# Forget sums and mask as a bias tile added with the maxima, and the gates' product between query chunks

## What is computed

```python
kvf = rmsnorm(h, kv_norm_g) @ w_kvf            # keys, values and 16 gate columns
log_f = log_sigmoid(kvf[..., 2 * D:] + b_f)
fcum = cumsum(transpose(log_f), axis=-1)       # (heads, tokens)
q = split_heads(rmsnorm(h, fox_pre_g) @ fox_w_q)
logits = q @ k.T / 8 + fcum[t] - fcum[s]       # masked to s <= t
h = h + rmsnorm(merge_heads(softmax(logits) @ v) @ fox_w_o, fox_post_g)
```

## Time and profile before

| | us |
|---|---|
| median of 3 runs (868.89 to 869.74) | 869.2 |
| the profiled execution | 869.43 |
| its span | 867.7 |
| PE busy | 853.5 (98%) |
| DVE busy | 677.7 (78%) |
| ACT busy | 524.2 (60%) |
| POOL busy | 65.3 (8%) |

### The profile page before, as it was taken

How to read it: one execution, slowest core, us unless ns; L and a number is a source line. 1 busy time by engine, 2 the same in 40 slices (tenths; PEclk the granted TensorE clock), 3 DMA queues, 4 the chain that set the end, 5 groups by cost and what they waited for, 6 DMA issues and landing times.

```text
span 867.7 us, 15051 instructions
## 1 busy us (share of the span) xinstructions
PE 853.5 (98%) x5782; PEld 750.6 (87%) x5782; DVE 677.7 (78%) x994; ACT 524.2 (60%) x766; POOL 65.3 (8%) x128
## 2 busy tenths in 40 slices
PE   8999999999999999999999999999999999999997
PEld 8999889888888889999898888888878779998885
DVE  5767569898887987566589878889888877699684
ACT  6666657765655774667486655656746757542552
POOL 2354100000000010010010000000000001000000
PEclk9999999999999999999999999999999999999999
DMA  8445335555545345424456465455263344462321
GB/s 298 189 148 188 119 124 197 216 186 204 192 161 225 146 159 206 146 98 146 146 206 242 147 224 207 150 202 187 101 224 136 115 141 150 156 229 88 122 97 48
DMA packets 21976, 144.62 MB, mean 167 GB/s; under 512 B 2831, under 2 KB 3103, under 8 KB 5280
## 3 DMA queue, kind: packets, MB, share of 16 engines
q1 hardware_dynamic: 20448, 139.47, 44.5%
q0 software_dynamic: 1328, 4.32, 1.6%
q10 hardware_dynamic: 144, 0.04, 0.0%
HBM read 142.78 MB, written 1.05 MB: 166 GB/s over the span
## 4 chain that ended last, share of the span: by engine, by line
PE 83%; DVE 9%; ACT 3%; issue 2%; DMA 1%; POOL 0%; SPq 0%; DVEq 0%; POOLq 0%; ACTq 0%
PE psC L2033 15%; PE psC L1941 11%; PE psC L1943 10%; PE psC L1942 10%; PE psC L2036 8%; PE psD L1941 5%; PE psD L1943 5%; PE psD L1942 5%; DVE w_lo L1116 2%; PE psC L2063 2%; PE psC L2065 2%; PE psC L2072 2%; DVE arena L1330 2%; DMA raw<-stream 1%; PE psD L2355 1%
## 5 line engine op out<-in xcount | busy, mean ns | idle before, releaser
L1116 DVE TENSOR_TENSOR w_lo<-raw,w_hi 128x2048 fp32r<-128x2048 f32 x125 | 285.7, 2287 | 54.1 <-ACT w_hi L561 53.3
L561 ACT ACTIVATE w_hi<-raw 128x2048 fp32r<-128x2048 f32 x125 | 238.4, 1911 | 65.2 <-PE psC L1943 31.7
L2033 PE MATMUL psC<-xT,w_hi 128*128 128x512 f32 x640 | 200.8, 395 | 0.0
L2036 PEld LDWEIGHTS psC<-xT,w_lo 128*128 128x128 f32 x640 | 120.2, 188 | 28.3
L2036 PE MATMUL psC<-xT,w_lo 128*128 128x256 f32 x640 | 125.7, 278 | 0.0
L2033 PEld LDWEIGHTS psC<-xT,w_hi 128*128 128x128 f32 x640 | 98.6, 189 | 1.2
L1941 PE MATMUL psC<-xT,w_hi 128*128 128x256 f32 x320 | 91.6, 286 | 0.0
L1942 PE MATMUL psC<-xT,w_hi 128*128 128x256 f32 x320 | 90.5, 283 | 0.0
L1943 PE MATMUL psC<-xT,w_lo 128*128 128x256 f32 x320 | 90.5, 283 | 0.0
L1941 PE MATMUL psD<-w_hi,oT_hi 128*128 128x512 f32 x208 | 81.4, 391 | 0.6 <-DVE oT_lo L1344 0.6
L1942 PE MATMUL psD<-w_lo,oT_hi 128*128 128x512 f32 x208 | 81.0, 389 | 0.0
(11 more groups left out here) (338 smaller groups left out, 1535.6 us busy)
## 6 DMA issues: line engine op xcount, KB each, us to landing
raw<-stream SPq DMA_DIRECT2D x130, 1024.0 KB, 4.8
gbc<-post_g POOLq DMA_DIRECT2D x6, 512.0 KB, 4.7
h<-x_in SPq DMA_DIRECT2D x2, 512.0 KB, 4.5
raw<-stream SPq DMA_DIRECT2D x4, 256.0 KB, 6.3
out<-h SPq DMA_DIRECT2D x3, 256.0 KB, 2.0
arena<-b_in POOLq DMA_DIRECT2D x1, 640.0 KB, 5.8
out<-h SPq DMA_DIRECT2D x2, 128.0 KB, 2.0
pv<-pvec POOLq DMA_DIRECT2D x1, 176.0 KB, 4.4
```

The source lines that it names most:

```text
L561: nc.scalar.activation(w_hi[:, slot, :], raw[:, raw_slot, :], ACT.Copy).then_inc(hi_done, 1)
L1116: V.tensor_tensor(w_lo[:, slot, :], raw[:, raw_slot, :], w_hi[:, slot, :].bitcast(F32), ALU.subtract).then_inc(lo_done, 1)
L2033: MM(psC[:, up_bank(e, a), :], hi[:, k, a * P:a * P + P], xT[:, kk_, :, :].rearrange("p i t -> p (i t)"), start=(kk_ == 0), stop=False, sk ...
L2036: ins = MM(psC[:, up_bank(e, a), 0:T], lo[:, k, a * P:a * P + P], xT[:, kk_, 0, :], start=False, stop=(kk_ == KT - 1), skip_group_check=True)
```

## The change

The forget sums no longer go through PE. DVE writes the negated sums of 16 rows to `ftmp`; POOL stores them to memory (`f_rows`) and spreads them with four transfers over all 128 partitions into `f_bias` (384 columns for each of 16 heads, 4 heads a transfer); the first 128 columns and the last 128 of each head are written with the triangle's mask by affine_select. DVE's pair_max then has one form: it waits for the logits and for the group's bias, reads the logits from PSUM, adds the bias tile and takes the maximum in one instruction, as in the window attention. ACT's take_logits, POOL's mask_logits and PE's forget_rows are gone, and with them the selection matrix, the second copy of the gate columns and the zeroing on POOL. The gates' product is moved ahead of the second query chunk. DVE makes `wf_lo` right after the spread of the scales, and the evacuation of the second query chunk comes behind the running sum; the splits move one unit around these steps. The logits' first matmul in a bank now starts the accumulation.

```diff
-        bf_sb = sb("bf_sb", [F2, 1])
+        bf_sb = sb("bf_sb", [H, 1])
+        wf_r = sb("wf_r", [P, 2, KT * H], F32R)
...
-        wf_sb = region(4608, KT * F2).rearrange("p (k n) -> p k n", k=KT)
-        o_flat = [a[:, :, :].rearrange("p k t -> p (k t)") for a in (oT_hi, oT_lo)]
-        wf_hi, wf_lo = (o_flat[1][:, KT * F2 * i:KT * F2 * (i + 1)].rearrange("p (k n) -> p k n", k=KT) for i in range(2))
-        sel = arena[:, 5632:7680].rearrange("p (h n) -> p h n", h=H)
-        ftmp = arena[0:F2, 8576:9344].rearrange("p (i t) -> p i t", t=T)
-
-
-        neg_f_all = o_flat[1][:, 6 * T:6 * T + P + T]
-        neg_f = neg_f_all[:, P:P + T]
-        sel_r = o_flat[0].rearrange("p (h n) -> p h n", h=H)
+        wf_sb = region(4608, KT * H).rearrange("p (k n) -> p k n", k=KT)
+        wf_hi, wf_lo = (wf_r[:, i, :].rearrange("p (k n) -> p k n", k=KT) for i in range(2))
+        ftmp = arena[0:H, 9984:10752].rearrange("p (i t) -> p i t", t=T)
+
+
+        f_bias = region(3840, 384 * H).rearrange("p (h n) -> p h n", h=H)
+        f_rows = nc.dram_tensor("f_rows", (H, T), F32, kind="Internal").ap()
...
-            nc.gpsimd.memset(wf_sb, 0.0).then_inc(pool_step, 1)
-            nc.gpsimd.memset(bf_sb[:, :], 0.0).then_inc(pool_step, 1)
...
-            nc.gpsimd.memset(sel, 0.0).then_inc(pool_step, 1)
...
-            for base in (0, -32):
-
-                keep(sel, ALU.not_equal, 1.0, base, [[-1, H], [0, P]], 1).then_inc(pool_step, 1)
-                done += 1
-                pool.wait_ge(pool_step, done)
...
-            def mask_logits(p):
-
-                pool.wait_ge(sm[0]["taken"], p + 1)
-                for a in (0, 2 * P):
-                    ins = keep(pair_p[p % 3][:, :, a:a + P], ALU.is_ge, NEG, 0, [[0, 2], [-1, P]], 1)
-                ins.then_inc(sm[0]["masked"], 1)
+            def forget_bias():
+
+                pool.wait_ge(forget["cum"], 1)
+                pool.dma_start(f_rows, ftmp[:, 2, :]).then_inc(forget["stored"], 16)
+                pool.wait_ge(forget["stored"], 16)
+                for g in range(4):
+                    heads_ = slice(4 * g, 4 * g + 4)
+                    pool.dma_start(f_bias[:, heads_, P:384], f_rows[heads_, :].partition_broadcast(P)).then_inc(forget_spread[g], 16)
+                for g in range(4):
+                    heads_ = slice(4 * g, 4 * g + 4)
+                    pool.wait_ge(forget_spread[g], 16)
+                    nc.gpsimd.affine_select(out=f_bias[:, heads_, 0:P], in_=f_bias[:, heads_, P:2 * P], compare_op=ALU.is_ge, fill=NEG,
+                                            base=0, pattern=[[0, 4], [-1, P]], channel_multiplier=1)
+                    keep(f_bias[:, heads_, 2 * P:384], ALU.is_ge, NEG, 0, [[0, 4], [-1, P]], 1).then_inc(forget["masked"], 1)
 
             for i in range(1, 4):
                 pre_scales(i)
                 next_gain(i)
                 if i == 2:
-                    for p in range(H // 2):
-                        mask_logits(p)
+                    forget_bias()
...
-            def take_logits(p):
-
-                s = sm[0]
-                act.wait_ge(s["logit"], p + 1)
-                if p >= 3:
-                    act.wait_ge(s["turned"], p - 2)
-                nc.scalar.activation(pair_p[p % 3], psD[:, 2 * (p % 2):2 * (p % 2) + 2, 0:384], ACT.Copy).then_inc(s["taken"], 1)
...
-            split_to(U0["fox_kv"] + 2)
-
-            act.wait_ge(unit_done, U0["fox_q"] + 4)
-            act.wait_ge(small_loaded, 16 * 6)
+            act.wait_ge(small_loaded, 16 * 4)
             nc.scalar.activation(wf_hi, wf_sb, ACT.Copy).then_inc(consts_act, 1)
-            act.wait_ge(consts_pool, N_CONSTS)
-            nc.scalar.activation(sel_r, sel, ACT.Copy).then_inc(forget["sel"], 1)
-            split_to(U0["fox_kv"] + 3)
+            split_to(U0["fox_kv"] + 1)
             act.wait_ge(forget["bias"], 1)
             settle(nc.scalar.activation(ftmp[:, 1, :], ftmp[:, 1, :], ACT.Exp, scale=-1.0))
             nc.scalar.activation(ftmp[:, 1, :], ftmp[:, 1, :], ACT.Ln, bias=1.0).then_inc(forget["ln"], 1)
...
-                dve.wait_ge(s["logit" if w else "masked"], p + 1)
+                dve.wait_ge(s["logit"], p + 1)
                 if w == 0:
-                    z = pair_p[p % 3]
-                    V.tensor_reduce(mx[:, w, pair, 0], z[:, :, 0:P], AX.X, ALU.max)
-                    settle(V.tensor_reduce(mx[:, w, pair, 1], z[:, :, P:384], AX.X, ALU.max))
-                    V.tensor_scalar(nmx[:, w, pair, :], mx[:, w, pair, :], -1.0, None, ALU.mult).then_inc(s["max"], 1)
-                    return
+                    dve.wait_ge(forget["masked"], p // 2 + 1)
                 if p >= 3:
                     dve.wait_ge(s["turned"], p - 2)
                 for r in range(2):
+                    i = 2 * p + r
                     for q, (a, b) in enumerate(((0, P), (P, 384))):
-                        ins = V.tensor_tensor_reduce(pair_p[p % 3][:, r, a:b], psD[:, at + r, a:b], mask_window[:, a:b], 1.0, NEG,
-                                                     ALU.add, ALU.max, accum_out=mx[:, w, 2 * p + r, q:q + 1])
+                        ins = V.tensor_tensor_reduce(pair_p[p % 3][:, r, a:b], psD[:, at + r, a:b],
+                                                     mask_window[:, a:b] if w else f_bias[:, i, a:b], 1.0, NEG,
+                                                     ALU.add, ALU.max, accum_out=mx[:, w, i, q:q + 1])
                 settle(ins)
+                if w == 0:
+                    V.tensor_scalar(nmx[:, w, pair, :], mx[:, w, pair, :], -1.0, None, ALU.mult).then_inc(s["max"], 1)
+                    return
...
+            dve.wait_ge(consts_act, 3)
+            V.tensor_tensor(wf_lo, wf_sb, wf_hi.bitcast(F32), ALU.subtract).then_inc(consts_dve, 1)
             split_to(U0["fox_q"] + 4)
             evac_features("fox_q", 0, qT, QSCALE)
-            split_to(U0["fox_kv"] + 2)
-            dve.wait_ge(consts_act, 3)
-            V.tensor_tensor(wf_lo, wf_sb, wf_hi.bitcast(F32), ALU.subtract).then_inc(consts_dve, 1)
-            evac_features("fox_q", 1, qT, QSCALE)
-            settle(V.tensor_scalar(neg_f_all, region(5632, 384), 0.0, None, ALU.mult))
-
+            split_to(U0["fox_kv"] + 1)
             dve.wait_ge(forget["product"], 1)
-            settle(V.tensor_tensor(ftmp[:, 0, :], psD[0:F2, 2, 0:T], scale_row[0:F2, :], ALU.mult))
+            settle(V.tensor_tensor(ftmp[:, 0, :], psD[0:H, 2, 0:T], scale_row[0:H, :], ALU.mult))
             settle(V.tensor_scalar(ftmp[:, 0, :], ftmp[:, 0, :], bf_sb[:, :], None, ALU.add))
             magnitude(ftmp[:, 1, :], ftmp[:, 0, :]).then_inc(forget["bias"], 1)
-            split_to(U0["fox_kv"] + 3)
+            split_to(U0["fox_kv"] + 2)
             dve.wait_ge(forget["ln"], 1)
             settle(V.scalar_tensor_tensor(ftmp[:, 2, :], ftmp[:, 0, :], 0.0, ftmp[:, 1, :], ALU.min, ALU.subtract))
-            settle(V.tensor_tensor_scan(ftmp[:, 1, :], ones_row[0:F2, :], ftmp[:, 2, :], 0.0, ALU.mult, ALU.add))
-            settle(V.tensor_scalar(neg_f[0:F2], ftmp[:, 1, :], -1.0, None, ALU.mult))
-            settle(V.scalar_tensor_tensor(neg_f[32:F2], ftmp[32:F2, 1, :], -1.0, neg_f[32:F2].bitcast(F32), ALU.mult, ALU.subtract))
-            V.tensor_copy(neg_f_all[0:F2, 0:P], neg_f[0:F2, 0:P].bitcast(F32)).then_inc(forget["cum"], 1)
+            settle(V.tensor_tensor_scan(ftmp[:, 1, :], ones_row[0:H, :], ftmp[:, 2, :], 0.0, ALU.mult, ALU.add))
+            V.tensor_scalar(ftmp[:, 2, :], ftmp[:, 1, :], -1.0, None, ALU.mult).then_inc(forget["cum"], 1)
+            evac_features("fox_q", 1, qT, QSCALE)
+            split_to(U0["fox_kv"] + 3)
             fox_keys(0)
             fox()
...
+            def forget_product():
+
+                pe.wait_ge(consts_dve, 2)
+                out = psD[0:H, 2, 0:T]
+                for b in range(4):
+                    pe.wait_ge(kv_hi_done, b + 1)
+                    for k in (2 * b, 2 * b + 1):
+                        MM(out, wf_hi[:, k, :], xT_hi[:, k, :], start=(k == 0), stop=False, skip_group_check=True)
+                        MM(out, wf_lo[:, k, :], xT_hi[:, k, :], start=False, stop=False, skip_group_check=True)
+                    pe.wait_ge(kv_lo_done, b + 1)
+                    for k in (2 * b, 2 * b + 1):
+                        ins = MM(out, wf_hi[:, k, :], xT_lo[:, k, :], start=False, stop=(k == KT - 1), skip_group_check=True)
+                ins.then_inc(forget["product"], 1)
...
-                def forget_rows(g):
-
+                def logits(g):
+
+                    pe.wait_ge(chunk_freed_v, V_FREED[e0 + 2 * g])
+                    if g:
+                        pe.wait_ge(s["pT"], 2 * g)
                     for p in (2 * g, 2 * g + 1):
-                        if g:
-                            pe.wait_ge(s["pT"], p - 1)
-                        for r, z in enumerate(logit_banks(p)):
```

(16 more changed lines are left out.)

40 lines of the change are left out of this document (12 added, 28 removed).

## The result

| | kernel before | changed kernel |
|---|---|---|
| median, 13 executions each | 869.18 (868.64 to 869.74) | 871.25 (869.80 to 872.27) |
| profiled execution | 869.43 | 870.26 |
| its span | 867.7 | 868.5 |

The ratio is 1.0022, with a 95% interval of 1.0015 to 1.0029: the changed kernel is 2.1 us slower. The forecast was 867.4 with a range of 866.3 to 869.8, so the sign and the range were both wrong.

The account below looks back on a forecast made before the run. PE, 98% busy, was taken as the bound. Forget rows -2.78, narrower product -0.05 and a new wait +1.03 gave -1.80 us, so 869.2 - 1.8 = 867.4 us, range 866.3 to 869.8.

Parts of the forecast that it names:

- What bounds it: PE, 98% busy; in each head group DVE, ACT and POOL must finish between logits and turning, 10.26 us in the first.
- Part 1: Sixteen forget-row matmuls leave PE's path: -2.78 us, bounds -2.7 and -3.2.
- Part 2: Gates' product on PE moves and its weights shrink from 48 to 16 columns: -0.05 us, bounds 0 and -0.2.
- Part 3: PE newly waits for DVE's wf_lo before the moved product: 0.95 us plus 0.08 restart, +1.03, bounds +0.6 and +1.3.
- The sum: PE's total over the stage: -2.78 - 0.05 + 1.03 = -1.80 us, if nothing else becomes late.
- Part 4: Bias tile's store, spread and masks: first group ready at 350.1, up to 352, before DVE could use it at 351.7.
- Part 5: First group's chain from logits to normalised probabilities takes 7.3 us, leaving 2.0 spare before PE's turning; costs and brings 0.
- rival (a): POOL's masks and DVE's split and normalisations hold each other up: about 868.5 us; chance 0.11.
- Part 6: Removed copies and zeroing, later bank release, splits and weight loads, and 2 MB of spreads: all at no cost.
- Rival (b): The bias tile's first spread lands late, only with the last; PE waits 4.5 us: 871.9 us; chance 0.12.

Follow-up runs that it names:

- the product at its old place: Changed kernel with bias tile stored and spread early from input x, and the gates' product back between the keys' first and second pieces: 866.48 us, ratio 0.9968.
- the early tile: Changed kernel with the bias tile stored and spread some 15 us earlier from rows of input x, output not the reference's: 867.15 us, ratio 0.9978.
- the sum first: Changed kernel with DVE's running sum of the gates moved ahead of the split of the second key/value unit: 867.0 us, ratio 0.9976.
- the loads held: Changed kernel with SP holding one weight load, and the next behind it, until the first spread has landed: 867.29 us, ratio 0.9979.

## Why the prediction was wrong, step by step

- **What bounds it** was right, and also that the distance from logits to turning in the first group is what decides. One reading was off: the normalisation that ends at 360.07 is the second pair's, and PE doesn't want it at 360.75, where the twelve turnings begin, but six turnings later (0.65 us, since twelve last 1.47 and one pitch is 0.108). So the spare was 1.3 us there and not 0.7.
- **Part 1** (forget rows, -2.78) was right: -2.7 with the product at its old place, and the groups that no tile holds up take 15.96 us each, where before three took 400.50 - 350.49 = 50.01, 16.67 each, 0.7 more.
- **Part 2** (-0.05) had its sign wrong, at no consequence: 24 matmuls from 327.71 to 330.51 are 2.80, pitch 0.117 (2.82 where nothing waits ahead of them, in the kernel with wf_hi and wf_lo made earlier), against 2.76 for 48 columns. Fewer columns of weights make no shorter pitch; the scaling from 128 over 48 to 16 columns had no ground.
- **Part 3** (+1.03) had the right mechanism: wf_lo on DVE started at 327.36 and took 0.29, and PE started at 327.71 (forecast 327.73). By starts its 0.95 was right too: from the eight matmuls ahead of the product (L2050) to the product it takes 327.71 - 325.81 = 1.90 in the changed kernel and 326.91 - 325.95 = 0.96 where wf_lo is early, 0.94 less. The 0.08 for a longer first matmul did not show: the product takes no more behind the wait (2.80) than without one (2.82). In the medians the wait is worth less: 0.7 between the kernels with and without it at the early tile, 867.0 - 866.36 = 0.6 between the two with the sum first. Where the other 0.2 to 0.3 went is not located; with 6 and 10 executions, the lowest and highest 0.5 to 1.0 apart, it can be noise.
- **The sum** -1.80 was right: the kernel with the early tile is at -2.1 against the kernel before beside it, and the one with the loads held at -1.9. By starts, from the eight matmuls ahead of the product to the last group's logits, it is 398.44 - 325.58 = 72.86 with the early tile against 400.50 - 325.82 = 74.68 before: -1.82. Parts 2 and 3 (the 0.08) were off by too little to matter.
- **Part 4** is the step that failed, in two terms. The store was priced by the output's 128 KB at 2.0, a transfer at the end of the kernel with no weight load beside it; here a weight load issued 1.5 us ahead of it was under way and it took 5.0 (2.5 with no load, 1.7 at the end of one). The first spread was priced by a gain at 4.7, which is what it took with the loads held, and had 7.0 to the masks' start, 2.3 of it from weight loads. So the tile was ready at 355.9 and not at 350.1, and PE waited 2.1 us at the first turnings where the forecast had a spare of 2.0. I had allowed 2 us for the pieces, which cost 0.7, and nothing for company. I had written that the spreads add at most two loads' worth of traffic and asked what they do to the loads, not what the loads do to them. The threshold looks good by luck: by it PE waits from a tile later than 353.7, so 2.2 us at 355.9, and 2.10 were measured. But with the early tile the second normalisation ends at 358.79, and PE wants it six turnings behind 360.81, at 361.46: the spare is 2.7 and not 2.0. The longer normalisation, which the forecast's case didn't have, took about as much back.
- **Part 5** (7.3 us) was right where no mask met it. In the changed kernel it is 364.08 - 356.08 = 8.0: the first normalisation is 0.65 longer. This is rival (a)'s mechanism. The Trainium skill, SBUF — State Buffer, "SBUF: two separate sides", states it as an exclusive lock, for a DVE operation with two SBUF inputs, of which no row had shown DVE's side; the trace agrees: a DVE operation that reads SBUF twice is held up by a POOL mask, 1.68 for 1.03, and is back at 1.03 when the mask is away.
- **Part 6** held: no split, load or bank was late in a way that PE saw. The loads did pay where the spreads went first (10.4 us for 4.8, with the sum ahead of the split), and PE had room for it.
- **Rival (b)** had the right sign, place and threshold (slower than before from a tile at 355.5; it came at 355.9) and nearly the right time (871.9), by another mechanism: the first spread did not end only with the last, it and the store were slowed by weight loads. "The weight load beside it is issued only [...] some 2 us behind it" stood there as evidence against. It left out the load beside the store; and since that made the spread late, the next load was issued 1.0 us ahead of the spread. It was true only where the store was quick: with the sum first, the load came 2.1 us behind the spread, and the masks started after 5.0. With 0.12 for it, the chance was far too low for a chain with two transfers in it, each priced from a row without company.
- **What no case had** is the clock: a wait of 2 us on PE costs up to 1.6 more behind it, by the times in about half of the executions (14 of 24 above 871). It turned a loss of 1.1 to 1.3 against before into 1.8 to 2.1.

## What to carry to other kernels

Where a small transfer stands in a dependency, ask what the big ones are doing at that moment: price its landing once alone and once beside a load, look which of the two is issued first, and move its source ahead of one split, or hold a load, if it would come second. Where a kernel keeps PE at the full clock, price a new idle stretch of PE at more than its length, and read the granted clock behind it in more than one execution. When a median lies well above the profiled execution, that difference is a finding of its own.
